# Loading x first and pooling between the convolution's taps in an encoder layer

## What is computed

```python
proj = x @ w_in[l]
u = proj[..., :POOL_CH]                               # 256 columns
v = proj[..., POOL_CH:POOL_CH + 2 * CONV_CH]          # 512 columns
q = proj[..., POOL_CH + 2 * CONV_CH:]                 # 512 columns
y_pool = pool_mixer(u, w_pool[l], pool_scale[l])
y_conv = conv_mixer(v, w_dw[l], b_dw[l], conv_norm_g[l], conv_norm_b[l])
y_mem = mem_attention(q, mem_n, w_kv[l])
mix = jnp.concatenate([y_pool, y_conv, y_mem], axis=-1) @ w_out[l]
x = layer_norm(DEEPNORM_ALPHA * x + mix, ln1_g[l], ln1_b[l])
ffn = moe(x, ...)                                     # 64 experts, top 8, and a shared one
x = layer_norm(DEEPNORM_ALPHA * x + ffn, ln2_g[l], ln2_b[l])
```

## Time and profile before

| what | us |
|---|---|
| median of 3 runs (1541.80 to 1545.91) | 1544.19 |
| the profiled execution | 1544.48 |
| its span, first to last instruction | 1542.9 |
| gate0's first matmul, from the span's start | 28.02 |
| a0's first matmul | 42.36 |
| mean's first matmul | 192.97 |
| the barrier behind the stage | 230.30 |
| TensorE busy, share of the span | 1395.5 (90%) |
| VectorE busy, share of the span | 1041.7 (68%) |

### The profile page before, as it was taken

How to read it: one execution, slowest core, us unless ns; L and a number is a source line. 1 busy time by engine, 2 the same in 40 slices (tenths; PEclk the granted TensorE clock), 3 DMA queues, 4 the chain that set the end, 5 groups by cost and what they waited for, 6 DMA issues and landing times.

```text
span 1542.9 us, 26021 instructions
## 1 busy us (share of the span) xinstructions
PE 1395.5 (90%) x6543; PEld 1133.9 (73%) x6544; DVE 1041.7 (68%) x1172; ACT 771.8 (50%) x1063; POOL 479.7 (31%) x462
## 2 busy tenths in 40 slices
PE   6976946699979999999999999999999999999784
PEld 5864736577767888888888888888888888888331
DVE  4399956367785377766579456555775797776287
ACT  3122145321233377757677565666775787675200
POOL 1049001126644233333333333333333333333011
PEclk9988977798869999999999999999999999999897
DMA  5112022222346689787689667657787898885995
GB/s 208 41 41 83 14 109 80 82 82 83 83 145 197 149 303 374 273 340 277 239 326 392 249 242 296 255 206 298 264 334 296 334 368 346 313 301 188 376 428 247
DMA packets 79458, 357.25 MB, mean 232 GB/s; under 512 B 22880, under 2 KB 22992, under 8 KB 50880
## 3 DMA queue, kind: packets, MB, share of 16 engines
q1 hardware_dynamic: 42416, 276.21, 47.4%
q0 software_dynamic: 35856, 76.41, 14.3%
q10 hardware_dynamic: 1152, 4.19, 0.7%
HBM read 324.01 MB, written 67.34 MB: 254 GB/s over the span
## 4 chain that ended last, share of the span: by engine, by line
PE 73%; DVE 15%; DMA 6%; issue 4%; ACT 2%; SPq 0%; POOLq 0%; POOL 0%; DVEq 0%; ACTq 0%
PE ps L1499 36%; PE ps L1517 17%; PE ps L1317 6%; DVE cv L940 5%; PE ps L1342 4%; DMA yg<-y_d 3%; PE ps L1431 2%; PE ps L1580 2%; PE ps L1535 1%; DVE acc L1294 1%; DVE whl L897 1%; PE ps L1389 1%; PE ps L1418 1%; DMA xg<-x_d 1%; DVE xres L1135 1%
## 5 line engine op out<-in xcount | busy, mean ns | idle before, releaser
L1499 PE MATMUL ps<-wgu,xTe 128*128 (+1 forms) x2496 | 596.0, 394 | 1.3 <-issue 0.9
L1499 PEld LDWEIGHTS ps<-wgu,xTe 128*128 128x128 f32 x2496 | 462.2, 189 | 94.7 <-issue 2.3
L586 POOL DMA_INDIRECT y_d<-ysb,idx x95 | 134.5, 1416 | 563.1 <-ACT ysb L799 507.2
L1199 DVE TENSOR_TENSOR wgu<-raw,wgu (+1 forms) x130 | 292.1, 2289 | 9.9 <-issue 9.8
L1517 PE MATMUL ps<-wdn,hT 128*128 (+1 forms) x1236 | 297.4, 389 | 0.0
L1517 PEld LDWEIGHTS ps<-wdn,hT 128*128 128x128 f32 x1236 | 231.9, 188 | 48.4 <-ACT hT L818 0.2
L742 ACT CAST wgu<-raw (+1 forms) x130 | 249.7, 1923 | 9.1 <-SPq L392 6.3
L1204 DVE TENSOR_TENSOR xTe<-ps,xTe 128x512 fp32r<-128x512 f32 x210 | 134.8, 683 | 133.1 <-ACT xTe L794 131.0
L1199 DVE TENSOR_TENSOR wdn<-raw,wdn (+1 forms) x65 | 149.0, 2292 | 44.4 <-ACT wdn L787 35.6
L799 ACT ACTIVATE ysb<-ps 128x512 f32<-128x512 f32 x204 | 110.9, 596 | 123.9 <-PE ps L1517 119.0
L787 ACT CAST wdn<-raw (+1 forms) x65 | 127.1, 1955 | 0.0
(11 more groups left out here) (204 smaller groups left out, 1239.5 us busy)
## 6 DMA issues: line engine op xcount, KB each, us to landing
raw<-in_w_gate SPq DMA_DIRECT2D x64, 1024.0 KB
raw<-in_w_up SPq DMA_DIRECT2D x64, 1024.0 KB
raw<-in_w_down SPq DMA_DIRECT2D x64, 1024.0 KB
yg<-y_d SPq DMA_DIRECT2D x8, 2048.0 KB, 28.6
yg<-y_d SPq DMA_DIRECT2D x16, 1024.0 KB, 32.6
wraw<-in_w_in SPq DMA_DIRECT2D x10, 512.0 KB, 3.6
xin<-in_x POOLq DMA_DIRECT2D x8, 512.0 KB, 4.9
wraw<-in_w_kv SPq DMA_DIRECT2D x8, 512.0 KB, 3.2
```

Of the source, the lines that this page charges most:

```text
L586: g.indirect_dma_start(out=y_d, out_offset=bass.IndirectOffsetOnAxis(ap=idx[:, c % RING, 1:2], axis=0), in_=ysb[:, c % 2], in_offset=None, ...
L1199: V.tensor_tensor(dst, raw_, hi.bitcast(F), ALU.subtract).then_inc(done, 1)
L1499: last = mm(ps[:, 2 + s, :], xTe[:, s, st, d], wgu[:, w, mo, d].rearrange("p a n -> p (a n)"), start=(d == 0 and st == 0 and mo == 0), sto ...
```

## The change

Three things, all in the projection stage:

1. All eight tiles of x are loaded by SyncE at the start, into eight buffers. These lie at 168.5 KB of SBUF, where cv, buf1, buf2 and diff are written later. The first weight's load stands behind the fourth tile; the memory tokens, the second and third weight and the small tables follow the last tile. GpSimd issues no load of x.
2. The transposes use four pairs of PSUM banks (in the order 0, 1, 2, 3, 0, 1, 3, 0) instead of two, so TensorE first waits for a pair at the fifth tile. ScalarE splits the first weight before the fifth tile, VectorE before the sixth, instead of ahead of all. gate0's first half (tokens 0 to 511) waits for four tiles only, its second for eight.
3. The pooling sums and means are done by VectorE in five parts, after its work at K2, K3, V0, V1 and V2. The multiplication by 1/window and the subtraction of the token are one operation there, and the sixteen end columns go through a small tile, ends8.

```diff
-        xin = at("xin", 124, [128, 3, D])
+        xin = at("xin", 168.5, [128, NT, D])
+        ends8 = at("ends8", 207.125, [128, 2, 16])
+        XBANKS = (0, 1, 2, 3, 0, 1, 3, 0)
...
         @block.sync
         def _(sp):
+            for t in range(NT):
+                sp.dma_start(xin[:, t], a["x"][t]).then_inc(s_x[t], 16)
+                if t == 3:
+                    project_weights(0)
+            for m in range(2):
+                sp.dma_start(memin[:, m], a["mem"][m]).then_inc(s_mem, 16)
+            project_weights(1)
+            project_weights(2)
             sp.dma_start(mgb[:], a["mem_gb"]).then_inc(s_par, 16)
...
         @block.gpsimd
         def _(g):
             g.memset(bd[:], 0.0).then_inc(s_const, 1)
-            for t in range(3):
-                g.dma_start(xin[:, t], a["x"][t]).then_inc(s_x[t], 16)
...
-            step(g.tensor_tensor(buf1[:, :, 0:W - 1], uP[:, :, 0:W - 1], uP[:, :, 1:W], ALU.add))
-            step(g.tensor_tensor(buf2[:, :, 0:W - 3], buf1[:, :, 0:W - 3], buf1[:, :, 2:W - 1], ALU.add))
...
         @block.vector
-            split_lo(0)
             for t in range(NT):
+                if t == 5:
+                    split_lo(0)
                 for b in range(2):
                     v.wait_ge(s_xhi, 2 * t + b + 1)
...
+            POOL_IN = ["K2", "K3", "V0", "V1", "V2"]
+            def mean_minus_token(grp, buf):
+                w = POOL_WINDOWS[grp]
+                p, c, lo = slice(64 * (grp % 2), 64 * (grp % 2) + 64), grp // 2, 8 - w // 2
+                step(V.scalar_tensor_tensor(diff[p, c, :], buf[p, c, lo:lo + S], 1.0 / w, uP[p, c, 8:8 + S],
+                                            ALU.mult, ALU.subtract))
+                ends = ((0, 0), (S - 8, 8))
+                for t0, e0 in ends:
+                    step(V.tensor_tensor(ends8[p, c, e0:e0 + 8], buf[p, c, lo + t0:lo + t0 + 8],
+                                         edge[p, c, e0:e0 + 8], ALU.mult))
+                settle()
+                for t0, e0 in ends:
+                    step(V.tensor_tensor(diff[p, c, t0:t0 + 8], ends8[p, c, e0:e0 + 8],
+                                         uP[p, c, 8 + t0:16 + t0], ALU.subtract))
...
+                if w in POOL_IN:
+                    pooling(POOL_IN.index(w))
...
         @block.tensor
-                pe.wait_ge(s_x[t % 3], 16 * (t // 3 + 1))
-                if t >= 2:
-                    pe.wait_ge(s_xlo, t - 1)
-                transpose_tile(xin[:, t % 3], 2 * (t % 2)).then_inc(s_xt, 1)
+                pe.wait_ge(s_x[t], 16)
+                if t >= 4:
+                    pe.wait_ge(s_xlo, max(u for u in range(t) if XBANKS[u] == XBANKS[t]) + 1)
+                transpose_tile(xin[:, t], 2 * XBANKS[t]).then_inc(s_xt, 1)
...
-                if w == "gate0":
-                    pe.wait_ge(s_xlo, NT)
...
                     for h in range(2):
+                        if w == "gate0":
+                            pe.wait_ge(s_xlo, NT // 2 * (h + 1))
```

More of the change, by code:

```diff
@@ L181, in build @@
         s_bd = sem("s_bd")
-        s_x = [sem(f"s_xin{i}") for i in range(3)]
+        s_x = [sem(f"s_xin{i}") for i in range(NT)]
         s_mem = sem("s_mem")
@@ L323, in _, with project_weights @@
         def _(sp):
+            def project_weights(n):
+                sp.dma_start(wraw[:, n % 3], w_src(n)).then_inc(s_w[n % 3], 16)
+            for t in range(NT):
[6 more added lines that the diff above has]
+            project_weights(2)
             sp.dma_start(mgb[:], a["mem_gb"]).then_inc(s_par, 16)
@@ L331, in _ @@
                 sp.dma_start(bd[o:o + 64, g // 2, o:o + 64], a["w_pool"][g]).then_inc(s_bd, 16)
[L332 to L338, removed]
+            for n in range(3, 18):
+                sp.wait_ge(s_wlo, n - 2)
+                project_weights(n)
             sp.wait_ge(s_wlo, 18)
@@ L636, in split_hi @@
                 nc.scalar.copy(whl[:, n % 2, 0], wraw[:, n % 3]).then_inc(s_whi, 1)
-            split_hi(0)
             for t in range(NT):
+                if t == 4:
+                    split_hi(0)
                 act.wait_ge(s_xt, t + 1)
@@ L922, in _, with pooling @@
                                 ALU.mult).then_inc(s_mln, 1)
+            POOL_IN = ["K2", "K3", "V0", "V1", "V2"]
+            W = S + 16
+            def mean_minus_token(grp, buf):
[11 more added lines that the diff above has]
+                                         uP[p, c, 8 + t0:16 + t0], ALU.subtract))
+            def pooling(part):
+                if part == 0:
+                    v.wait_ge(s_u, 2)
+                    v.wait_ge(s_const, 8)
+                    step(V.tensor_tensor(buf1[:, :, 0:W - 1], uP[:, :, 0:W - 1], uP[:, :, 1:W], ALU.add))
+                elif part == 1:
+                    settle()
+                    step(V.tensor_tensor(buf2[:, :, 0:W - 3], buf1[:, :, 0:W - 3], buf1[:, :, 2:W - 1], ALU.add))
+                    mean_minus_token(0, buf1)
+                elif part == 2:
+                    settle()
+                    step(V.tensor_tensor(buf1[:, 1, 0:W - 7], buf2[:, 1, 0:W - 7], buf2[:, 1, 4:W - 3], ALU.add))
+                    mean_minus_token(1, buf2)
+                elif part == 3:
+                    settle()
+                    mean_minus_token(2, buf1)
+                    step(V.tensor_tensor(buf2[:, 1, 0:W - 15], buf1[:, 1, 0:W - 15], buf1[:, 1, 8:W - 7], ALU.add))
+                else:
+                    settle()
+                    mean_minus_token(3, buf2)
+                    settle()
+                    v.sem_inc(s_diff, 1)
             kvhi = tap = 0
```

32 lines of the change are left out of this document (2 added, 30 removed).

## The result

| | before | changed |
|---|---|---|
| median of the timed runs, same chip | 1545.05 us (1541.8 to 1548.44, 4 runs) | 1528.11 us (1526.86 to 1530.52, 4 runs) |
| profiled execution, its span | 1544.48, 1542.9 us | 1527.39, 1525.8 us |
| gate0 starts | 28.02 | 16.99 |
| K0's matmuls start | 104.17 | 91.51 |
| q0's matmuls start | 153.37 | 135.05 |

What follows compares the result with a forecast made beforehand. It took gate0's start and VectorE's stretch from 104.03 us to its last tap as bounding the part the change touches: 1544.48 - 12.4 (x first) - 2.6 (pooling on VectorE) = 1529.5 us, range 1524 to 1538.

Steps and rivals of the forecast that it cites:

- The front: Loading and transposing x before the first projection: gate0 starts at 17.1, a0 at 29.9, 12.4 us gained.
- The clock's part: TensorE at gate0: idle before it is some 0.2 us, so gate0 takes 11.0 instead of 12.59, gaining 1.5 us.
- The rival with transposes at 1.95 all along: TensorE stays at 1.2 GHz through x's transposes: gate0 at 20.3, 4.7 us less gained, 1534.2; chance 0.12.
- The stretching: VectorE's taps and weight splits beside GpSimd's pooling last 19.2 us longer; with pooling on VectorE this goes.
- The pooling's cost: Pooling sums, means and small operations on VectorE take 14.7 us, all in line.
- The half-rate rival: The four fused pooling operations on VectorE take 2.22 us each instead of 1.20: 4.1 more, 1533.6; chance 0.01.
- The waits: VectorE's waits from K0 to its last tap: 6.2 us, the largest 3.7 for q2's weight.
- 37.3 us that the change does not touch: The stretch from the LayerNorm mean to the barrier at the mixer's end, taken to last 37.3 us as before.
- K and V jobs: Rival: these matmul jobs run at 2.4 GHz, x0 may land at 4.2; about 2.5 us more gained, 1527; chance 0.14.
- The tiles of x landed in order: Against the rival that x shares bandwidth with all 13 transfers: gate0 near 28, only 2.6 us gained, 1541.9; chance 0.05.
- the dear small operations: Rival: the pooling's small operations on VectorE cost GpSimd's 0.69 us each: 8.4 more, 1537.9; chance 0.03.
- stretching that stays whole: Slower rival: VectorE's 19.2 us come from TensorE's reads or DMA and stay: 5.3 us slower, 1549.8; chance 0.03.

Runs made afterwards that it cites:

- e3: The kernel before with pooling sums and means left out (diff zeroed): mean at 177.88 us, barrier at 218.18; its total of 1547.36 is not comparable.
- e12: The changed kernel run once more, same program: 1526.79 us, ratio 0.9875.
- e1: The changed kernel with the pooling put back on GpSimd, new front kept: 1533.85 us, ratio 0.9935.
- e10: The kernel before with only the first weight's load moved to the head of SyncE's queue: gate0 starts at 28.91 us.
- e7: The changed kernel with the first weight loaded and split ahead of all tiles of x: gate0 starts at 16.96 us.
- e8: The changed kernel with the eight tiles of x issued by GpSimd on its own queue: gate0 starts at 21.90 us.
- e2: The kernel before with only the pooling moved to VectorE, old front kept: 1541.54 us, ratio 0.9973.
- e4: The changed kernel with pooling sums and means left out (diff zeroed): mean at 162.25 us, barrier at 201.29; its total of 1534.96 is not comparable.
- e6: The changed kernel with the transposes through two pairs of PSUM banks instead of four: gate0 starts at 18.62 us.

## Why the prediction was right

| step | predicted | measured |
|---|---|---|
| first transposes | 4.6 | 4.41 |
| interval of the late tiles | 1.28 | 1.28 |
| gate0 | 17.1 | 16.99 |
| gate0's duration | 11.0 | 10.93 |
| a0 | 29.9 | 29.66 |
| pooling on VectorE | 14.7 | 13.5 |
| VectorE's waits | 6.2 | 3.85 |
| VectorE's stretch from K0 to its last tap | 86.2 | 83.1 |
| mean | 178 | 174.63 |
| mean to barrier | 37.3 | 40.3 |
| barrier | 215 | 214.94 |
| total | 1529.5 | 1528.11 (profiled 1527.39) |

- **The front** came out as laid out, through two errors that offset each other. From 4 to 6 us the transfers moved less than the 410 GB/s of the earlier trace rows, and less than from 17 to 20 (the last figure of a row):

```profile
4.00:6.00 2.00, 1.59 (x8) 1.63 (x9) 0.00 (x0) 0.00 (x0) 0.00 (x0) 1.00 0.82 305
17.00:20.00 3.00, 3.00 (x14) 2.46 (x14) 3.00 (x6) 1.37 (x3) 0.00 (x0) 1.00 1.04 382
```

so x7 landed at 15.85, not 14.8. The wait for x4's pair of PSUM banks, which I had put last at 15.7, was over at 15.08. What ended last was the landing; the mechanism I named for the last tile was the wrong one. The clock's part was right: no gap was over 1.05 us and gate0 ran at the 2.4 GHz level throughout. The rival with transposes at 1.95 all along fell: only the first tiles took that.
- **The stretching** went entirely, as forecast; e3 shows its cause. The 19.2 us of longer instructions were a fair count, though only 16.5 of them lay on the path.
- **The pooling's cost** was 1.2 us too high. Parts: 2.23, 3.78, 2.97, 2.79 and 1.68, together 13.5. The wide sums and the fused operations were as sized (2.23 and 1.13 to 1.22 in the chain); two small ones follow each other in 0.17 to 0.26 where I had taken 0.30. The half-rate rival fell, at 1.22 us for an operation it would put at 2.22. Here the rule of the Trainium skill, Vector Engine (DVE) Microarchitecture Reference, section Points that are easy to get wrong, that this form with two non-bf16 SBUF sources halves throughput, is not borne out.
- **The waits** were the step that failed: 3.85 instead of 6.2. They are

```profile
DVE kT L986 <- ACT kT L642: 1.8, 1, 1.8
```

that is 1.8 for K0's result (I had 1.4), 0.52 for K1's weight, 0.16 for an own result ahead of q0's split, and

```profile
151.74 1.23 DVE L872 TENSOR_TENSOR whl<-wraw,whl 128x1024 fp32r<-128x1024 f32 x1 [1.35 <-ACT whl L610]
```

1.35 at q2's weight, where I had 3.7. I had set q0's matmuls behind V3's taps. They start behind VectorE's split alone:

```profile
133.68 1.23 DVE L872 TENSOR_TENSOR whl<-wraw,whl 128x1024 fp32r<-128x1024 f32 x1 [0.16 <-DVE diff L914]
134.82 2.48 DVE L958 SCALAR_TENSOR_TENSOR cv<-glu,wdw,cv 128x1024 f32<-128x1024 f32 x2
```

The split ends at 134.91 and q0 starts at 135.05, with two taps (to 137.3) still to come. So TensorE is 2.4 us further on than I had it, and VectorE has eleven taps to do beside q0 and not nine. The trace of before had it already. VectorE's two taps there, and its waits for weight casts from 75 to 193 us (total, count, longest):

```profile
153.15 2.47 DVE L940 SCALAR_TENSOR_TENSOR cv<-glu,wdw,cv 128x1024 f32<-128x1024 f32 x2
```

```profile
DVE whl L897 <- ACT whl L636: 3.2, 2, 1.8
```

The taps run to 155.62, and q0 starts at 153.37. And the second of the two waits, the one at q2's weight, is 1.36 us, behind the same q0 stretch that the change leaves alone; the prediction names it ("another such wait at q2's weight") and then puts 3.7 in its place. I should have looked at the starts of both engines' rows at one job before adding up the order. Of the 3.1 us by which this stretch was too long in the forecast, 2.35 are these waits and 1.2 the pooling's cost, with 0.4 of small pieces the other way.
- From q0's start to the mean it is 39.60 before, 39.58 after, 39.61 in e12 and 39.60 in e1: one fixed sequence of q0, pooling jobs, a copy, the split of q2's weight and seventeen taps. Hence the gain of K0 to q0 arrives at the mean undiminished, and TensorE's wait before the mean is 3.25 in all of them.
- **"37.3 us that the change does not touch"** was wrong by 3.0. No instruction there was moved, but the clock was another: 6.64 us for the mean at a granted 0.55. With the same wait of 3.25 before it, the mean took 3.67 (before, e10), 5.1 to 5.4 (e12, e7, e8, e1, e2, e4) and 6.6 to 6.7 (changed, e3, e6). 3.67 is the best case, not the usual one, and the profile of before happened to show it. Whether the change makes the slower cases more frequent isn't settled by one profile of each kernel: e10, whose front and pooling are those of before, had 3.67 too, but e3, also with the old front, 6.60.
- **The other rivals.** K and V jobs did not come to run at the 2.4 GHz level throughout: the granted clock is 0.80 from K0 to q0, and was 0.81 before. The tiles of x landed in order. The small operations cost 0.16 us and not GpSimd's 0.69. Three sums of the prediction are slightly off and change nothing: its waits add up to 6.1, not 6.2; the dear small operations come to 8.6 more, not 8.4; and stretching that stays whole would make 19.2 - 15.0 = 4.2 us slower, not 5.3, by its own turning point.

So -12.7, -5.7, +2.9 and -1.7 behind the barrier make -17.1. The forecast's -12.4 and -2.6 were short by 0.3 and 3.1; the clock took 2.9 of that back. The mechanism of both parts was right but for what ends last at x7, and the front's size too. That the total of 1529.5 was good to 1.4 us is luck in so far as the 3.1 us of the waits and the pooling and the 2.9 us of the clock, neither of them foreseen, cancel.

## What to carry to other kernels

When an operation is moved between VectorE and GpSimd, price it on the path with and without it on either engine: 16.5 us on GpSimd and 11.6 on VectorE here, for 13.5 us of work, so moving it won 4.9 to 5.7 and not the 19 of the longer instructions. When several things hold a start (a weight, buffers, banks), removing the one that the chain names can give nothing (e10) and another's order can be free (e7). What decided here was the last byte to land, and it came forward by 4.9 us when everything the start needs, and nothing else, stood in front on one queue (e8). A wait of TensorE of a few us can have a price behind it besides its length, and a stage that no edit touches can change by it. A gain of 1 to 3 us in one stage must be read in that stage: the stages behind it differ by as much from one execution to the next.

## What the runs showed of the hardware that was not expected

- The same wait of 3.25 us is followed by 3.67 to 6.72 us for the same eight matmuls, in one program too (6.64 in the changed kernel, 5.18 in e12). A wait of 2.5 before q0 was followed by 1.4 to 1.6 us of extra time in four of five kernels, waits up to 1.4 in none.
- The first transfers are slower than the later ones on the same queue: 305 GB/s from 4 to 6 us, 382 from 17 to 20. With both queues at work from 4 to 6 us it is 360 in the kernel before and 363 in e8.
- The first tile of x lands at 8.8 us when GpSimd issues it beside SyncE's weights (e8), at 5.9 beside SyncE's small tables (before), and at 4.4 when SyncE issues it in front.
- The same instructions behind the barrier took 1310.1 to 1315.3 us in twelve profiles.
- A matmul job's start is set by the split in front of VectorE's taps and not by the taps: TensorE works ahead of what VectorE's list still holds.
